# Row gathers that name fixed index columns instead of copied ones, in a hybrid attention, delta-rule and expert layer

## Chip, cores and metric

One NeuronCore of a Trainium2 chip. The metric is the device time of the program in microseconds (us). The engines are TensorE (PE), VectorE (DVE), ScalarE (ACT), GpSimd (POOL) and SyncE (SP); transfers run on 16 DMA engines.

## What is computed

One layer over 1024 tokens of width 1024, in fp32: layer norm; a mixing part (sliding-window attention and a gated delta rule) with a residual and a second layer norm; then a sparse expert part, and a last layer norm. The expert part is what the change touches. For each token it picks 8 x 16 = 128 rows out of 16384, takes those rows of `expert_u` for dot products with the token, and adds the same rows of `expert_v` with the results as weights:

```python
expert = i1 * N_KEYS + i2                     # (tokens, 8 heads, 16)
gates = jax.nn.softmax(best, axis=-1)
...
u = jnp.take(expert_u, et, axis=0)            # (128 tokens, 128 slots, 1024)
act = jax.nn.gelu(jnp.einsum('tkd,td->tk', u, xt), approximate=False) * gt
return jnp.einsum('tk,tkd->td', act, jnp.take(expert_v, et, axis=0))
```

Each row is 4 KB, so a token reads 1 MB and all 1024 tokens read 1.07 GB.

## The kernel before

The tokens are cut into T = 8 tiles of P = 128, one token a partition. A first stage (up to about 540 us) makes the first layer norm and the input projections of all tiles. A second stage then does for each tile the mixing part and the routing, in NPIECE = 49 pieces, and the gathers of its expert rows. The pieces of tile t + 1 are dealt out between the gathers of tile t, engine by engine, by tables written out by hand (`VECTOR_AT`, `TENSOR_AT`, `SCALAR_AT`); the pieces of tile 0 run alone ahead of the first gather (at about 617 us), and the last tile's gathers run with no pieces beside them.

A tile has SLOTS = 128 rows for each token, in NGROUP = 32 groups of GS = 4. One gather (`indirect_dma_start`) is issued by POOL and reads one row for each of 128 tokens, 512 KB. There are four buffers for U rows and four for V rows. In step s POOL issues, for k = 0 to 3 in turn, the U gather of group s and the V gather of group s - 1 into buffer k (L822, L827), each behind a wait until the buffer is free (`g_ufree[k]` at L820, `g_vfree[k]` at L825). DVE makes the dot product of each U row with the token (L1708), which frees the U buffer; ACT makes the gelu of the four dots (L1292) and frees the fourth; DVE multiplies with the gate (L1722). The V rows are added by weight: in most groups buffers 0 and 1 by PE, with diagonal matrices that ACT writes (L1286, L1130), and buffers 2 and 3 by DVE (L1714). Who adds a row frees its buffer. Each engine runs its instructions in the order in which they are written.

The indices of a tile are made by DVE in the last piece (n == 48), which waits for `g_indexfree`, writes `eidx_n` and raises `g_tile`. POOL (`next_tile`, L846) waits for `g_tile`, copies `eidx_n` to `eidx` (L849) and raises `g_indexfree`. A gather takes its index column from a small buffer: ahead of each step POOL copies four columns of `eidx` to `ixu` (L831) and the four of the group before to `ixv` (L834), waiting for each copy. The steps run in a loop over j with two steps in its body (L841) inside a loop over tiles (L859). At the end of a tile the last V columns are copied (L862), then the new tile's list (L849), then its first U columns (L853).

Of the kernel before, what the change touches and what calls it, by code (L numbers as in the profile page):

```python
# [17 lines left out]
P = 128  # L18
S = 1024
D = 1024  # L20
T = S // P
# [6 lines left out]
SLOTS = PH * TOPK  # L28
# [10 lines left out]
GS = 4  # L39
NGROUP = SLOTS // GS  # L40
# [72 lines left out]
def build(nc, consts, x, ln_in_g, ln_in_b, w_in, conv_w, a_sinks, b_a_log, b_dt_bias, b_norm_w, w_out,  # L113
          ln1_g, ln1_b, w_query, sub_keys, expert_u, expert_v, ln2_g, ln2_b, out):
    fp32, u32 = mybir.dt.float32, mybir.dt.uint32
# [3 lines left out]
    with ctx:  # L119
        def sb(name, shape, dt=fp32, c=ctx):  # L120
            return c.enter_context(nc.sbuf_tensor(name, shape, dt))
# [3 lines left out]
        def sem(name):  # L125
            return scope[0].enter_context(nc.semaphore(name))
# [4 lines left out]
        s_pool = sem("s_pool")  # L131
# [446 lines left out]
        b = ExitStack()  # L578
# [54 lines left out]
        eidx_n = sb("eidx_n", [P, SLOTS], u32, c=b)  # L633
        egate_n = sb("egate_n", [P, SLOTS], c=b)

        U = sb("U", [P, GS, D], c=b)
        V = sb("V", [P, GS, D], c=b)
        eidx = sb("eidx", [P, SLOTS], u32, c=b)
        egate = sb("egate", [P, SLOTS], c=b)
        ixu = sb("ixu", [P, 2, GS], u32, c=b)  # L640
        ixv = sb("ixv", [P, 2, GS], u32, c=b)
        dots = sb("dots", [P, 2, GS], c=b)
        gl = sb("gl", [P, 2, GS], c=b)
        dg = sb("dg", [P, 2, GS, P], c=b)
# [86 lines left out]
        g_u = [sem(f"g_u{k}") for k in range(GS)]  # L731
        g_v = [sem(f"g_v{k}") for k in range(GS)]
        g_ufree = [sem(f"g_ufree{k}") for k in range(GS)]
        g_vfree = [sem(f"g_vfree{k}") for k in range(GS)]
# [27 lines left out]
        rows = bass.IndirectOffsetOnAxis  # L762

        with nc.Block() as block:
# [48 lines left out]

            @block.gpsimd
            def _(pool):
                def fetch(par, u, v):

                    for k in range(GS):
                        if u:
                            pool.wait_ge(g_ufree[k], 1)  # L820
                            pool.sem_inc(g_ufree[k], -1)  # L821
                            pool.indirect_dma_start(U[:, k, :], None, expert_u[0],  # L822
                                                    rows(ap=ixu[:, par, k:k + 1], axis=0)).then_inc(g_u[k], 16)
                        if v:
                            pool.wait_ge(g_vfree[k], 1)  # L825
                            pool.sem_inc(g_vfree[k], -1)
                            pool.indirect_dma_start(V[:, k, :], None, expert_v[0],  # L827
                                                    rows(ap=ixv[:, 1 - par, k:k + 1], axis=0)).then_inc(g_v[k], 16)

                def step(s, par):  # L830
                    nc.gpsimd.tensor_copy(ixu[:, par, :], eidx[:, bass.ds(s * GS, GS)]).then_inc(s_pool, 1)  # L831
                    pool.wait_ge(s_pool, 1)
                    pool.sem_inc(s_pool, -1)  # L833
                    nc.gpsimd.tensor_copy(ixv[:, 1 - par, :], eidx[:, bass.ds(s * GS - GS, GS)]).then_inc(s_pool, 1)  # L834
                    pool.wait_ge(s_pool, 1)
                    pool.sem_inc(s_pool, -1)
                    fetch(par, True, True)

                def steps():

                    with pool.Fori(0, NGROUP // 2 - 1) as j:  # L841
                        step(2 * j + 1, 1)
                        step(2 * j + 2, 0)
                    step(NGROUP - 1, 1)

                def next_tile():  # L846
                    pool.wait_ge(g_tile, 1)
                    pool.sem_inc(g_tile, -1)  # L848
                    nc.gpsimd.tensor_copy(eidx[:, :], eidx_n[:, :]).then_inc(s_pool, 1)  # L849
                    pool.wait_ge(s_pool, 1)  # L850
                    pool.sem_inc(s_pool, -1)
                    pool.sem_inc(g_indexfree, 1)
                    nc.gpsimd.tensor_copy(ixu[:, 0, :], eidx[:, 0:GS]).then_inc(s_pool, 1)  # L853
                    pool.wait_ge(s_pool, 1)
                    pool.sem_inc(s_pool, -1)

                next_tile()
                fetch(0, True, False)
                with pool.Fori(0, T - 1) as t:  # L859
                    steps()  # L860

                    nc.gpsimd.tensor_copy(ixv[:, 1, :], eidx[:, SLOTS - GS:SLOTS]).then_inc(s_pool, 1)  # L862
                    pool.wait_ge(s_pool, 1)
                    pool.sem_inc(s_pool, -1)
                    next_tile()
                    fetch(0, True, True)
                steps()
                nc.gpsimd.tensor_copy(ixv[:, 1, :], eidx[:, SLOTS - GS:SLOTS]).then_inc(s_pool, 1)
                pool.wait_ge(s_pool, 1)
                pool.sem_inc(s_pool, -1)  # L870
                fetch(0, False, True)

            @block.tensor
            def _(pe):
# [1012 lines left out]
```

## Time and profile before

| | us |
|---|---|
| median of 3 runs | 4302.2 (4296.01 to 4318.66) |
| span of the profiled execution | 4299.7 |
| DVE, PE, POOL, ACT busy | 2684.1, 2796.3, 2539.3, 652.9 |
| gathers on POOL: 1024 U, 1024 V | 1189.4 and 1151.0 busy |
| copies on POOL | 187 busy |
| DVE waited for U rows | 737.9, in 442 waits |

The span is what the profiler saw from the first to the last instruction of one execution. Views of this execution show groups of instructions by source line (busy time, mean, idle time ahead of them and what ended it), waits by releaser, the instructions in order of time, and busy time by stretch. On POOL, "issue" as releaser means that nothing that the profile shows was waited for, and "POOLq L821" that the last thing ahead was a row of POOL's own sequencer at that line, a semaphore wait included.

### The profile page before, as it was taken

The page shows a single profiled execution, that of the slowest core. Times are in us where ns is not written, and L with a number is a line of the kernel's source. Part 1 is how long each engine was busy: PE and PEld are TensorE (multiplying, and loading weights), DVE is VectorE, ACT ScalarE, POOL GpSimd, SP SyncE. Part 2 cuts the span into 40 slices and gives each one's busy share as a digit, 9 for nine tenths or more (in the row PEclk, how much of TensorE's full clock was granted, in tenths as well). Part 3 has the DMA queues.
Part 4 walks back from the last instruction along what each step waited for, and adds up shares of the span by engine and source line. Part 5 has one row for each costly group of instructions (what it writes and reads, how often), then busy time and mean ns, then how long its engine had stood idle before and what let it go on. Part 6 is the DMA issues. An engine that isn't in the chain of part 4 may idle for free. (4 is left out here: it accounts for less than half of the span.)

```text
span 4299.7 us, 36977 instructions
## 1 busy us (share of the span) xinstructions
PE 2796.3 (65%) x8621; PEld 1470.1 (34%) x8621; DVE 2684.1 (62%) x5500; ACT 652.9 (15%) x1407; POOL 2539.3 (59%) x2582
## 2 busy tenths in 40 slices
PE   5997726676567656675567657765666566764444
PEld 2444523342244324242334224332434233521111
DVE  3121267677666867586766766686768776776555
ACT  2122102111211112111211121111211121111000
POOL 1000017667666766677667766676667766777775
PEclk9998767788777878788788867787878877887666
DMA  3224128888888888888888888888898888889997
GB/s 118 73 78 161 58 78 309 307 309 290 307 294 310 307 308 291 317 306 293 306 308 294 300 304 294 309 305 304 288 330 314 294 306 313 304 300 319 321 317 268
DMA packets 365654, 1172.84 MB, mean 273 GB/s; under 512 B 45285, under 2 KB 86294, under 8 KB 364442
## 3 DMA queue, kind: packets, MB, share of 16 engines
q0 software_dynamic: 294912, 1073.87, 71.3%
q1 hardware_dynamic: 66090, 81.05, 5.6%
q10 hardware_dynamic: 4464, 15.76, 1.0%
q8 instruction: 75, 1.23, 0.1%
q14 instruction: 113, 0.93, 0.1%
HBM read 1150.59 MB, written 19.96 MB: 272 GB/s over the span
## 5 line engine op out<-in xcount | busy, mean ns | idle before, releaser
L1130 PE MATMUL bank<-V,dg 128*128 128x512 f32 x2412 | 1518.5, 787 | 1168.8 <-PEq L1123 822.2
L1708 DVE CUSTOM_DVE_ANT_0 U<-U,h1c 128x1024 f32<-128x1024 f32 x1024 | 1253.2, 1227 | 933.4 <-DMA U<-in_expert_u,ixu 737.9
L827 POOL DMA_INDIRECT V<-in_expert_v,ixv x1024 | 1151.0, 1124 | 568.6 <-POOLq L821 296.5
L822 POOL DMA_INDIRECT U<-in_expert_u,ixu x1024 | 1189.4, 1161 | 493.2 <-issue 202.8
L1130 PEld LDWEIGHTS bank<-V,dg 128*128 128x128 f32 x2412 | 578.1, 253 | 2060.5 <-issue 1537.6
L1714 DVE SCALAR_TENSOR_TENSOR acc<-V,gl,acc 128x1024 f32<-128x1024 f32 x421 | 540.2, 1283 | 69.1 <-DMA V<-in_expert_v,ixv 61.0
L849 POOL COPY eidx<-eidx_n 128x128 uint32<-128x128 uint32 x8 | 4.2, 529 | 567.2 <-POOLq L848 566.9
L1286 ACT ACTIVATE dg<-C,gl 128x128 f32<-128x128 f32 x603 | 202.1, 392 | 683.5 <-ACTq L1284 615.4
L1292 ACT ACTIVATE gl<-dots 128x4 f32<-128x4 f32 x256 | 52.6, 206 | 1663.4 <-ACTq L1290 1652.7
L425 PE MATMUL bank<-hT,wbuf 128*128 128x512 f32 x704 | 304.1, 595 | 0.0
L970 PE MATMUL bank<-arena,wq 128*128 128x128 f32 x2048 | 255.5, 290 | 14.8 <-PEq L1104 8.9
L970 PEld LDWEIGHTS bank<-arena,wq 128*128 128x128 f32 x2048 | 251.3, 206 | 20.0 <-issue 19.7
L425 PEld LDWEIGHTS bank<-hT,wbuf 128*128 128x128 f32 x704 | 134.3, 191 | 169.0 <-issue 169.0
L379 DVE SCALAR_TENSOR_TENSOR ybuf<-bank,cw,ybuf 128x1023 f32<-128x1023 f32 (+2 forms) x36 | 46.1, 1281 | 201.0 <-DVEq L377 195.2
L945 PE MATMUL bank<-wo,arena 128*128 128x512 f32 x224 | 116.4, 664 | 25.5 <-PEq L1083 24.2
L834 POOL COPY ixv<-eidx 128x4 uint32 (+1 forms) x248 | 87.9, 354 | 69.5 <-POOLq L833 53.7
L1292 ACT ACT_TABLE_LOAD x50 | 64.2, 1283 | 209.3 <-ACTq L1290 206.6
L831 POOL COPY ixu<-eidx 128x4 uint32 (+1 forms) x248 | 91.4, 368 | 1.0
L1708 DVE DVE_READ_ACCUMULATOR2_ANT dots<- 128x1 f32 x1024 | 84.0, 82 | 0.0
L893 PE MATMUL bank<-raw 128*128 128x128 f32 x256 | 60.8, 325 | 27.5 <-PEq L890 22.4
L945 PEld LDWEIGHTS bank<-wo,arena 128*128 128x128 f32 x224 | 45.7, 211 | 85.2 <-issue 84.1
L894 PE MATMUL bank<-raw 128*128 128x128 f32 x320 | 67.1, 309 | 6.8 <-issue 3.4
(253 smaller groups left out, 2408.4 us busy)
## 6 DMA issues: line engine op xcount, KB each, us to landing
wo<-in_w_out SPq DMA_DIRECT2D x56, 512.0 KB
U<-in_expert_u,ixu POOLq DMA_INDIRECT x1024
V<-in_expert_v,ixv POOLq DMA_INDIRECT x1024
proj_dram<-obuf ACTq DMA_DIRECT2D x21, 512.0 KB, 2.6
raw<-proj_dram SPq DMA_DIRECT2D x8, 1344.0 KB
wbuf<-in_w_in SPq DMA_DIRECT2D x18, 512.0 KB, 3.8
wq<-in_w_query SPq DMA_DIRECT2D x4, 2048.0 KB, 18.0
xin<-in_x SPq DMA_DIRECT2D x8, 512.0 KB, 5.4
```

The costliest lines, as they stand in the source:

```text
L425: last = nc.tensor.matmul(banks[u][:, 512 * half:512 * half + 512], wbuf[:, u, k, :], hT[:, k, 512 * half:512 * half + 512], start=k == 0, ...
L822: pool.indirect_dma_start(U[:, k, :], None, expert_u[0], rows(ap=ixu[:, par, k:k + 1], axis=0)).then_inc(g_u[k], 16)
L827: pool.indirect_dma_start(V[:, k, :], None, expert_v[0], rows(ap=ixv[:, 1 - par, k:k + 1], axis=0)).then_inc(g_v[k], 16)
L831: nc.gpsimd.tensor_copy(ixu[:, par, :], eidx[:, bass.ds(s * GS, GS)]).then_inc(s_pool, 1)
L834: nc.gpsimd.tensor_copy(ixv[:, 1 - par, :], eidx[:, bass.ds(s * GS - GS, GS)]).then_inc(s_pool, 1)
L945: return nc.tensor.matmul(b0[:, 512 * n:512 * n + 512], yT[:, k, :], w[:, 512 * n:512 * n + 512], start=k == 0, stop=k == KD - 2)
L970: last = nc.tensor.matmul(o, wq[:, k, i * P:(i + 1) * P], h1T[:, k, :], start=k == 0, stop=k == KD - 1)
L1130: ins = nc.tensor.matmul(acc_ps[:, 512 * n:512 * n + 512], dg[:, 1 - par, k, :], V[:, k, 512 * n:512 * n + 512], start=first and k == 0, s ...
L1286: nc.scalar.activation(dg[:, 1 - par, k, :], ident, ACT.Copy, scale=gl[:, 1 - par, k:k + 1]).then_inc(g_diag, 1)
L1292: nc.scalar.activation(gl[:, par, :], dots[:, par, :], ACT.Gelu).then_inc(g_gelu, 1)
L1708: return nc.vector.tensor_tensor_reduce(out=U[:, k, :], in0=U[:, k, :], in1=h1c[:, :], scale=1.0, scalar=0.0, op0=ALU.mult, op1=ALU.add, a ...
L1714: return nc.vector.scalar_tensor_tensor(out=acc[:, :], in0=V[:, k, :], scalar=gl[:, 1 - par, k:k + 1], in1=acc[:, :], op0=ALU.mult, op1=AL ...
```

## The change

`eidx` gets two halves by tile, and each gather names its column of `eidx` itself. The buffers `ixu` and `ixv` and all copies into them go. For the column to be a fixed address, a tile's 31 steps after the first are written out, and the loop over tiles becomes one over pairs of tiles (`T // 2 - 1` = 3 turns) whose body holds two tiles with the halves 1 and 0. The order of the gathers, the waits for free buffers and the semaphores they raise are the same.

```diff
-        eidx = sb("eidx", [P, SLOTS], u32, c=b)
+        eidx = sb("eidx", [P, 2, SLOTS], u32, c=b)
-        ixu = sb("ixu", [P, 2, GS], u32, c=b)
-        ixv = sb("ixv", [P, 2, GS], u32, c=b)
...
-                def step(s, par):
-                    nc.gpsimd.tensor_copy(ixu[:, par, :], eidx[:, bass.ds(s * GS, GS)]).then_inc(s_pool, 1)
-                    pool.wait_ge(s_pool, 1)
-                    pool.sem_inc(s_pool, -1)
-                    nc.gpsimd.tensor_copy(ixv[:, 1 - par, :], eidx[:, bass.ds(s * GS - GS, GS)]).then_inc(s_pool, 1)
-                    pool.wait_ge(s_pool, 1)
-                    pool.sem_inc(s_pool, -1)
-                    fetch(par, True, True)
...
+                def u_row(e, s, k):
+                    pool.wait_ge(g_ufree[k], 1)
+                    pool.sem_inc(g_ufree[k], -1)
+                    c = s * GS + k
+                    pool.indirect_dma_start(U[:, k, :], None, expert_u[0],
+                                            rows(ap=eidx[:, e, c:c + 1], axis=0)).then_inc(g_u[k], 16)
...
+                def next_tile(e):
                     pool.wait_ge(g_tile, 1)
                     pool.sem_inc(g_tile, -1)
-                    nc.gpsimd.tensor_copy(eidx[:, :], eidx_n[:, :]).then_inc(s_pool, 1)
+                    nc.gpsimd.tensor_copy(eidx[:, e, :], eidx_n[:, :]).then_inc(s_pool, 1)
                     pool.wait_ge(s_pool, 1)
                     pool.sem_inc(s_pool, -1)
                     pool.sem_inc(g_indexfree, 1)
-                    nc.gpsimd.tensor_copy(ixu[:, 0, :], eidx[:, 0:GS]).then_inc(s_pool, 1)
-                    pool.wait_ge(s_pool, 1)
-                    pool.sem_inc(s_pool, -1)
...
+                def tile_rows(e):
+                    for s in range(1, NGROUP):
+                        for k in range(GS):
+                            u_row(e, s, k)
+                            v_row(e, s - 1, k)
+
+                def tile_after(e):
+                    next_tile(e)
+                    for k in range(GS):
+                        u_row(e, 0, k)
+                        v_row(1 - e, NGROUP - 1, k)
+                    tile_rows(e)
+
+                next_tile(0)
+                for k in range(GS):
+                    u_row(0, 0, k)
+                tile_rows(0)
+                with pool.Fori(0, T // 2 - 1):
+                    tile_after(1)
+                    tile_after(0)
+                tile_after(1)
+                for k in range(GS):
+                    v_row(1, NGROUP - 1, k)
```

## Rows read from the trace of the kernel before

**Rows 1.** The page's DMA queues: packets, MB, share of 16 engines' span.

```profile
q0 software_dynamic: 294912, 1073.87, 71.3%
```

**Rows 2.** Busy time by stretch: length, engines' busy us (instructions), PE's clock, DMA share, GB/s.

```profile
2463.00:2932.00 469.00, 311.67 (x982) 166.46 (x981) 323.00 (x673) 73.25 (x169) 314.39 (x321) 0.78 0.87 301
2932.00:3391.00 459.00, 302.11 (x984) 161.62 (x983) 322.85 (x674) 73.44 (x169) 316.00 (x321) 0.81 0.88 309
3849.00:4260.00 411.00, 188.11 (x263) 71.53 (x262) 236.53 (x350) 31.77 (x97) 304.77 (x311) 0.70 0.90 316
```

**Rows 3.** Timeline in the last tile: start, us, instruction, idle time before and releaser.

```profile
4099.91 0.19 POOL L831 COPY ixu<-eidx 128x4 uint32 x1
4100.35 0.19 POOL L834 COPY ixv<-eidx 128x4 uint32 x1 [0.24 <-POOLq L833]
4101.44 1.08 POOL L822 DMA_INDIRECT U<-in_expert_u,ixu  x1 [0.90 <-POOLq L826]
...
4104.14 1.20 POOL L822 DMA_INDIRECT U<-in_expert_u,ixu  x1 [0.30 <-issue]
...
4105.65 0.93 POOL L827 DMA_INDIRECT V<-in_expert_v,ixv  x1 [0.30 <-issue]
4106.57 1.22 DVE L1708 CUSTOM_DVE_ANT_0 U<-U,h1c 128x1024 f32<-128x1024 f32 x1 [0.83 <-DMA U<-in_expert_u,ixu]
4106.88 1.73 POOL L822 DMA_INDIRECT U<-in_expert_u,ixu  x1 [0.30 <-issue]
...
4110.15 0.94 POOL L822 DMA_INDIRECT U<-in_expert_u,ixu  x1 [0.30 <-issue]
...
4110.42 1.22 DVE L1708 CUSTOM_DVE_ANT_0 U<-U,h1c 128x1024 f32<-128x1024 f32 x1 [2.55 <-DMA U<-in_expert_u,ixu]
...
4112.46 0.20 POOL L831 COPY ixu<-eidx 128x4 uint32 x1
...
4113.03 1.23 DVE L1708 CUSTOM_DVE_ANT_0 U<-U,h1c 128x1024 f32<-128x1024 f32 x1 [1.37 <-DMA U<-in_expert_u,ixu]
```

**Rows 4.** Waits in the last tile, 3849 to 4260 us: total, times, longest.

```profile
DVE U L1708 <- DMA U<-in_expert_u,ixu: 152.9, 93, 3.2
```

**Rows 5.** Groups on POOL in the last tile: busy us, mean ns | idle before, releasers.

```profile
L822 POOL DMA_INDIRECT U<-in_expert_u,ixu x125 | 156.5, 1252 | 57.3 <-POOLq L826 27.8 <-issue 27.7 <-POOLq L821 1.8
L827 POOL DMA_INDIRECT V<-in_expert_v,ixv x124 | 135.2, 1090 | 42.1 <-issue 32.6 <-POOLq L821 7.4 <-POOLq L826 2.1
L831 POOL COPY ixu<-eidx 128x4 uint32 (+1 forms) x31 | 7.5, 241 | 0.1
L834 POOL COPY ixv<-eidx 128x4 uint32 (+1 forms) x31 | 7.3, 236 | 7.5 <-POOLq L833 6.8 <-issue 0.7
```

**Rows 6.** Groups on POOL in the middle tile, 2463 to 2932 us.

```profile
L827 POOL DMA_INDIRECT V<-in_expert_v,ixv x128 | 148.3, 1158 | 81.4 <-POOLq L821 45.5 <-issue 33.2 <-POOLq L826 2.7
L822 POOL DMA_INDIRECT U<-in_expert_u,ixu x128 | 144.8, 1131 | 63.4 <-issue 26.5 <-POOLq L821 20.4 <-POOLq L826 16.2
L831 POOL COPY ixu<-eidx 128x4 uint32 (+1 forms) x31 | 11.5, 371 | 0.1
L834 POOL COPY ixv<-eidx 128x4 uint32 (+1 forms) x31 | 9.2, 295 | 8.8 <-POOLq L833 6.8 <-issue 2.0
L849 POOL COPY eidx<-eidx_n 128x128 uint32<-128x128 uint32 x1 | 0.3, 289 | 0.3 <-POOLq L848 0.3
L862 POOL COPY ixv<-eidx 128x4 uint32<-128x4 uint32 x1 | 0.2, 191 | 0.0
L853 POOL COPY ixu<-eidx 128x4 uint32<-128x4 uint32 x1 | 0.2, 186 | 0.2 <-POOLq L851 0.2
```

**Rows 7.** Waits in the middle tile: total, times, longest.

```profile
DVE U L1708 <- DMA U<-in_expert_u,ixu: 86.6, 47, 6.2
POOL V L827 <- POOLq L821: 45.5, 18, 7.0
DVE U L1708 <- issue: 11.1, 11, 6.9
```

**Rows 8.** Timeline in the first tile: a V gather that waits for its buffer.

```profile
765.72 0.94 POOL L827 DMA_INDIRECT V<-in_expert_v,ixv  x1 [6.67 <-POOLq L821]
```

**Rows 9.** The stretch of 25 us in the last tile that moved most.

```profile
3882.00:3907.00 25.00, 13.34 (x21) 4.82 (x19) 15.66 (x22) 3.04 (x8) 17.59 (x19) 0.73 0.96 343
```

**Rows 10.** Timeline of DVE at its loop over tiles: the first dot after the jump.

```profile
2519.99 1.23 DVE L1708 CUSTOM_DVE_ANT_0 U<-U,h1c 128x1024 f32<-128x1024 f32 x1 [6.93 <-issue]
```

More of the change, by code:

```diff
@@ L815, in _ @@
             def _(pool):
[L816 to L828, printed above, removed]
@@ L830, in step @@
-                def step(s, par):
-                    nc.gpsimd.tensor_copy(ixu[:, par, :], eidx[:, bass.ds(s * GS, GS)]).then_inc(s_pool, 1)
-                    pool.wait_ge(s_pool, 1)
-                    pool.sem_inc(s_pool, -1)
-                    nc.gpsimd.tensor_copy(ixv[:, 1 - par, :], eidx[:, bass.ds(s * GS - GS, GS)]).then_inc(s_pool, 1)
-                    pool.wait_ge(s_pool, 1)
-                    pool.sem_inc(s_pool, -1)
-                    fetch(par, True, True)
[L839 to L844, printed above, removed]
@@ L846, in next_tile, with v_row @@
-                def next_tile():
+                def u_row(e, s, k):
[4 more added lines that the diff above has]
+                                            rows(ap=eidx[:, e, c:c + 1], axis=0)).then_inc(g_u[k], 16)
+                def v_row(e, s, k):
+                    pool.wait_ge(g_vfree[k], 1)
+                    pool.sem_inc(g_vfree[k], -1)
+                    c = s * GS + k
+                    pool.indirect_dma_start(V[:, k, :], None, expert_v[0],
+                                            rows(ap=eidx[:, e, c:c + 1], axis=0)).then_inc(g_v[k], 16)
@@ L852, in next_tile @@
                     pool.sem_inc(g_indexfree, 1)
-                    nc.gpsimd.tensor_copy(ixu[:, 0, :], eidx[:, 0:GS]).then_inc(s_pool, 1)
-                    pool.wait_ge(s_pool, 1)
-                    pool.sem_inc(s_pool, -1)
[L857 to L871, printed above, removed]
+                def tile_rows(e):
[19 more added lines that the diff above has]
+                    v_row(1, NGROUP - 1, k)
             @block.tensor
```

## The prediction

> **What bounds the kernel now.** Read first the page's queue line: the gathers of expert rows move 1073.87 MB on queue q0, whose packets take 71.3% of the sixteen DMA engines' span [rows 1]. Then the busy table by stretch [rows 2]: seven tiles (617 to 3849 us) run gathers beside the next tile's mixing and routing, the eighth (3849 to 4260 us) runs gathers alone. In neither does an engine look full: in a middle tile of 469 us DVE is busy 323.0, POOL 314.4, PE 311.7, the DMA engines 0.87; in the last tile DVE has 236.5 of 411 and the DMA engines 0.90. But POOL is fuller than its busy time says. In the timeline of the last tile [rows 3] each gather runs 0.93 to 1.73 us and the next begins 0.30 us behind it, released by nothing ("issue"). Behind the fourth V gather come the two index copies, 0.24 us apart, and behind them 0.90 us, not 0.30, until the next U gather. So POOL is never free there, and DVE waits for rows: 152.9 us in 93 waits in the last tile [rows 4]. There POOL sets the pace: the group period is 411/31 = 13.26 us; 4 x 1.252 + 4 x 1.090 = 9.37 in gathers [rows 5], 8 x 0.30 = 2.40 in gaps, 1.32 for the copies (below), 13.09 together, 0.17 left for true waits.
>
> In the seven overlapped tiles it is shared. In the middle tile POOL's gathers take 148.3 + 144.8 = 293.1 us, the idle time ahead of them 81.4 + 63.4 = 144.8 [rows 6]. Of this 256 x 0.30 = 77 is the fixed gap and 32 x 0.60 = 19 is what the copies add to theirs, which leaves 49 us in which POOL waited for a buffer to be freed; 45.5 us of the idle time stands under one releaser ahead of V gathers [rows 7]. A plain case is the V gather that starts at 765.72 after 6.67 us [rows 8]: PE frees V buffers 0 and 1 and was at work on the next tile. DVE, in turn, waited 86.6 us for U rows in this tile [rows 7]. So the chain goes back and forth: POOL, transfer, DVE or PE, buffer free, POOL.
>
> **What is removed, and its cost.** Per group: two copies of 128x4 with their semaphore waits. In the middle tile 0.371 + 0.295 = 0.67 us of copies, 8.8/31 = 0.28 between them [rows 6], and 0.90 - 0.30 = 0.60 of longer gap [rows 3]: 1.55 us a pair. In the last tile 0.241 + 0.236 = 0.48, 7.5/31 = 0.24 [rows 5], and 0.60: 1.32. At a tile boundary three copies become one: the copy from L862 (0.2) and the one from L853 (0.2 and 0.2 of idle) go too [rows 6], about one pair more, so I count 32 pairs for each of the seven tiles and 31 for the last. If all of it were on the path: 224 x 1.55 + 31 x 1.32 = 388 us. That is the ceiling, and not the forecast.
>
> **Last tile.** POOL's period without the pair is 13.26 - 1.32 = 11.94 us. The next thing that is late is the transfer. A group moves 8 x 0.524 = 4.19 MB; the stretch ran at 316 GB/s with share 0.90 [rows 2], which is 351 GB/s at share 1, hence 11.95 us a group. The best 25 us in it had 343 GB/s at 0.96 [rows 9], 357 at share 1. A queue that must be always full costs something, so I take 0.98 of 351: 12.2 us. The time from the start of a U gather to its dot says the same: 5.13, 6.28 and 6.15 us in one group [rows 3], it grows within a group, and the copies' pause lets it recover. Gain 13.26 - 12.2 = 1.06 us, x 31 = 33 us. Bounds: 31 x 0.4 = 12 (the ceiling of rival 2) and 31 x 1.32 = 41.
>
> **The seven tiles.** What counts are the pairs on the chain. I followed it back through the timelines of POOL, DVE and PE from the last gather of each tile: along POOL while a gather starts at its fixed gap (0.30, or 0.90 behind the copies, as in [rows 3]); over to the engine that frees the buffer where it starts later (as in [rows 8]); from DVE or PE back to POOL where a dot or a product had waited for its rows (the dots at 4106.57 and 4110.42 in [rows 3] are such). It crosses 83 of the 224 pairs, between 7 and 17 in a tile. A pair on the chain is worth less than 1.55: a copy alone needs 0.19 to 0.20 [rows 3], so 0.67 - 0.39 = 0.28 us of a pair is stretching. DVE work beside it is the likely reason: the gather at 4106.88 ran 1.73 us with a dot already running, the one at 4110.15, where the dot began after it, 0.94 [rows 3]. Without copies about half of this falls on the gather that comes there instead; I take 1.40. 83 x 1.40 = 116 us. Then chains that run close beside take over, and the transfer queue fills: 0.87 of the 469 us tile is 408 us of DMA time, and shortened by 17 us the tile is at 0.90, the share at which the last tile runs; this costs a part of it. I take three quarters, 87 us. Bounds: 83 x 1.55 = 129 above if my count is right, and a third (30 us) below; if the count is short by half, 190.
>
> **What is added and moved.** The second index buffer alternates by tile, so the copy from L849 stays, eight times, 0.29 us each [rows 6]; its wait is that of before. What is queued behind it on POOL is the new tile's first U gather and the old tile's last V gathers, on which DVE and PE wait; DVE hands over the list at the same place in its own order, and L849 had 0.3 us of idle time ahead of it [rows 6], so if POOL comes earlier than DVE this wait grows by at most the about 1.5 us that one group gained: 7 x 0 to 1.5, cost 0 to 10, and I take 0, since DVE comes earlier too. The order and number of gathers, and of every DMA, is the same; SP's, ACT's and PE's queues aren't touched.
>
> The code of POOL grows from a loop over two groups to one over two tiles, walked three times, with two jumps back over 512 gathers. No row of POOL shows such a jump. The nearest is DVE's own loop over the tiles, whose first dot after the jump stood 6.93 us for "issue" [rows 10]. For POOL: 2 x 0 to 7 us, part of it behind gathers already in its queue; I take 5 in all. The Trainium skill, page "Runtime: NRT & Kernel Launch", section "Instruction fetch mechanics", says that a sequencer fetches ahead in sequence and that a taken branch to a target outside its window of two blocks stalls it for a fetch; by that rule the change trades a loop that stays inside the window for one that doesn't, and straight code costs nothing. The row of the jump agrees with it; that straight code is free on POOL, no row shows.
>
> **Sum.** Against the profiled span of 4299.7, which stands 2.5 us (0.06%) below the median of 4302.2: -87 - 33 + 5 = -115. From the median: **4187 us**, 2.7% less.
>
> **Rivals.**
> 1. More pairs pass on (chance 0.17). The chain has many near equals, and POOL's earlier issue may lift waits that my walk gives to DVE or PE. For it: DVE's 86.6 us of waits in a tile of which I use 12. Against: POOL waits 49 us for buffers. 130 of 224 pairs at 1.40 is 182, with the last tile 33: 215 less 5, 4092.
> 2. The transfer, or DVE and PE, take over at once (0.19). If 325 GB/s is what random rows give when asked without pause, the last tile's period is 13.26 x 316/325 = 12.89, a gain of 11 us, and the tiles, at 301 to 309 GB/s already, keep a third of mine, 30: 4302 - 41 + 5 = 4266. For it: share 0.87 to 0.90 now. Against: 343 GB/s in 25 us.
> 3. No change that can be told (0.08): all of the seven tiles' pairs are hidden and the last tile gives 11: 4291. The form in which the change does not do what it says would land here too: copies left in the code. The diff leaves one per tile, so I give that nothing of its own.
> 4. Slower (0.06): POOL stands at blocks of straight code as DVE does at its jump. One stop of 6.93 us [rows 10] in every eight groups is 32 x 6.93 = 222 us against a gain of 115: 4409. It decides from 3.6 us a stop on (115/32). Against: of DVE's 11 "issue" waits in the middle tile, 11.1 us in all, the longest is 6.9 [rows 7], so its hundreds of straight instructions cost at most 4.2 us a tile.
>
> **How the numbers follow.** My forecast (4150 to 4225) has 0.50, the rivals 0.17, 0.19, 0.08 and 0.06. A measurement of this kernel can tell about 0.5%, 21.5 us, from no change. Faster by more: 0.50 + 0.17 + 0.19 = 0.86; same 0.08; slower 0.06. The range takes in the first rival up to its own value and most of the second's: 4095 to 4268, and leaves out the ends.
>
> **What would show it.** Copies on POOL: 8, no more. Gaps ahead of all U gathers 0.30 as ahead of V gathers; group period in the last tile about 12.2, DMA share there 0.97 or more, GB/s near 343; time from U gather to dot longer than 6.3 us there. In a middle tile about 450 us, DVE's waits for U rows down from 86.6 to about 75, and POOL's true waits up from 49 us to about 80. Two stops of POOL at the new jump. I am wrong if POOL's gathers get longer by more than 0.15 us, if "issue" gaps of microseconds stand on POOL away from the jump, or if the last tile keeps its 13.26 us.

## The result

The changed kernel took 4183.81 us (median, 4181.41 to 4185.75) against 4299.1 us for the kernel before (its fourth run lowers the 4302.2 that stands ahead): ratio 0.9727, with a 95% interval of 0.97 to 0.9754, in which the quotient of the two medians, 0.9732, lies too. The prediction said 4187. The profiled execution has a span of 4179.9 us, 119.8 less than before.

Groups of the page of the changed kernel (busy us, mean ns | idle before, releaser), for the whole execution:

```profile
L1695 DVE CUSTOM_DVE_ANT_0 U<-U,h1c 128x1024 f32<-128x1024 f32 x1024 | 1252.3, 1226 | 825.3 <-DMA U<-in_expert_u,eidx 609.3
L825 POOL DMA_INDIRECT V<-in_expert_v,eidx x1024 | 1166.9, 1140 | 768.0 <-POOLq L816 480.5
L818 POOL DMA_INDIRECT U<-in_expert_u,eidx x1024 | 1211.8, 1183 | 396.3 <-issue 244.2
L831 POOL COPY eidx<-eidx_n 128x128 uint32<-128x128 uint32 x8 | 2.4, 297 | 564.9 <-POOLq L830 564.9
```

Eight copies are left on POOL. The same dots on DVE, 1252 us of them, waited 609.3 us for U rows where it had been 737.9, and POOL stands 768.0 us ahead of V gathers where it had stood 568.6.

Busy time by stretch of the changed kernel, two overlapped tiles and the last one (columns as in [rows 2], which they answer):

```profile
2844.00:3293.00 449.00, 294.02 (x980) 158.30 (x980) 321.85 (x673) 73.25 (x169) 294.37 (x257) 0.82 0.87 314
3293.00:3740.00 447.00, 300.06 (x981) 161.40 (x981) 320.73 (x672) 73.34 (x169) 295.59 (x257) 0.81 0.87 312
3741.00:4139.00 398.00, 184.41 (x264) 70.35 (x263) 238.36 (x351) 31.75 (x97) 306.04 (x248) 0.71 0.91 327
```

POOL in the last tile of the changed kernel, to set against [rows 5]:

```profile
L818 POOL DMA_INDIRECT U<-in_expert_u,eidx x124 | 159.5, 1286 | 40.4 <-issue 32.3 <-POOLq L816 5.9 <-POOLq L823 2.1
L825 POOL DMA_INDIRECT V<-in_expert_v,eidx x124 | 146.9, 1185 | 52.6 <-issue 30.2 <-POOLq L816 20.9 <-POOLq L823 1.5
```

And POOL in the middle tile (2394 to 2843 us), to set against [rows 6], with DVE's wait there against [rows 7]:

```profile
L818 POOL DMA_INDIRECT U<-in_expert_u,eidx x128 | 144.9, 1132 | 52.1 <-issue 29.0 <-POOLq L816 17.1 <-POOLq L823 6.1
L825 POOL DMA_INDIRECT V<-in_expert_v,eidx x128 | 143.7, 1123 | 108.6 <-POOLq L816 65.4 <-issue 28.6 <-POOLq L823 14.6
```

```profile
DVE U L1695 <- DMA U<-in_expert_u,eidx: 69.7, 36, 6.5
```

The reader is to see two things. In the middle tile the gathers are as long as they were (288.6 us, 293.1 before) and their idle time is 160.7 us; less 77 of fixed gaps, POOL now waits 84 us for free buffers where it had waited 49. So 35 us of the 50 that the copies gave back there (32 x 1.55) went into such waits. In the last tile the gathers themselves are longer: 1.236 us in the mean, 1.171 before.

To compare kernels, the table gives for each profiled execution the time from the first U gather of tile 0 to that of tile 7 (seven tiles), and from there over the next 31 groups (last tile). The letters stand for chips. B and C are two different ones; C was used twice, once before B and once after it. Of A, where the pair of the result ran, it isn't known which chip it was, and it may be B. A and B gave the changed kernel the same ratio; C did not, and that matters below. Each stretch in the table is of one execution; equal copies in the last tile of two kernels on C gave 408.8 and 417.9 us there, so differences of a few us between such stretches say little.

| kernel | chip | median us | ratio to before (95%) | seven tiles | last tile |
|---|---|---|---|---|---|
| before | A | 4299.1 | 1 | 3231.8 | 410.8 |
| changed | A | 4183.81 | 0.9727 (0.97 to 0.9754) | 3124.7 | 398.7 |
| changed again | B | 4185.49 | 0.9707 (0.9674 to 0.974) | 3131.4 | 393.4 |
| unused buffers | B | 4182.82 | 0.9704 (0.9668 to 0.974) | 3128.1 | 394.0 |
| last-tile copies, moved | B | 4193.1 | 0.9732 (0.9702 to 0.9761) | 3120.0 | 408.3 |
| short dots | B | 3952.1 | 0.9178 (0.9144 to 0.9212) | 2922.2 | 358.6 |
| changed, third time | C | 4301.44 | 0.9932 (0.9908 to 0.9957) | 3242.5 | 397.8 |
| written out, with copies | C | 4292.54 | 0.9931 (0.9911 to 0.9951) | 3208.7 | 418.5 |
| copies without drain | C | 4312.11 | 0.9975 (0.9949 to 1.0) | 3253.7 | 402.4 |
| the same, moved | C | 4310.93 | 0.9968 (0.9943 to 0.9993) | 3258.5 | 401.6 |
| last-tile copies | C | 4322.87 | 0.9998 (0.9975 to 1.002) | 3252.0 | 408.8 |
| the same again | C | 4327.1 | 1.0 (0.997 to 1.003) | 3256.7 | 417.9 |
| one copy, looped | C | 4259.5 | 0.9862 (0.9813 to 0.9911) | 3187.9 | 401.0 |
| four U, then four V | C | 4419.09 | 1.023 (1.0184 to 1.0276) | 3307.4 | 445.8 |

The kernel before took 4310.85 us on B, and 4322.65 and 4327.98 on C beside the two sets of runs.

### The profile page after: what moved, and what is told of

Its sections match the earlier page's. It is cut to its first block and busy times, and to the rows that moved or that the text cites. A ratio compares the mean times of both kernels' runs of the same rounds, so it can differ in the third digit from the quotient of the medians.

```text
span 4179.9 us, 35217 instructions
## 1 busy us (share of the span) xinstructions
PE 2734.9 (65%) x8621; PEld 1444.9 (35%) x8621; DVE 2681.4 (64%) x5500; ACT 653.2 (16%) x1407; POOL 2392.1 (57%) x2070
## 5 line engine op out<-in xcount | busy, mean ns | idle before, releaser
L1117 PE MATMUL bank<-V,dg 128*128 128x512 f32 x2412 | 1474.0, 767 | 1131.5 <-PEq L1110 866.1
L1695 DVE CUSTOM_DVE_ANT_0 U<-U,h1c 128x1024 f32<-128x1024 f32 x1024 | 1252.3, 1226 | 825.3 <-DMA U<-in_expert_u,eidx 609.3
L825 POOL DMA_INDIRECT V<-in_expert_v,eidx x1024 | 1166.9, 1140 | 768.0 <-POOLq L816 480.5
L818 POOL DMA_INDIRECT U<-in_expert_u,eidx x1024 | 1211.8, 1183 | 396.3 <-issue 244.2
L1117 PEld LDWEIGHTS bank<-V,dg 128*128 128x128 f32 x2412 | 565.3, 247 | 1992.8 <-issue 1772.6
L831 POOL COPY eidx<-eidx_n 128x128 uint32<-128x128 uint32 x8 | 2.4, 297 | 564.9 <-POOLq L830 564.9
L1695 DVE DVE_READ_ACCUMULATOR2_ANT dots<- 128x1 f32 x1024 | 84.1, 82 | 0.0
L881 PE MATMUL bank<-raw 128*128 128x128 f32 x320 | 67.2, 309 | 6.8 <-PEq L877 6.8
L1667 DVE TENSOR_TENSOR arena<-arena 128x800 f32<-128x800 f32 x64 | 63.5, 992 | 9.4
L1670 DVE TENSOR_REDUCE arena<-arena 128x16 f32<-128x800 f32 x64 | 63.1, 986 | 9.3
```

Of the source, the lines that this page charges most:

```text
L818: pool.indirect_dma_start(U[:, k, :], None, expert_u[0], rows(ap=eidx[:, e, c:c + 1], axis=0)).then_inc(g_u[k], 16)
L825: pool.indirect_dma_start(V[:, k, :], None, expert_v[0], rows(ap=eidx[:, e, c:c + 1], axis=0)).then_inc(g_v[k], 16)
L881: last = nc.tensor.matmul(g[2][:, h * P:(h + 1) * P], Pm[:, h, :], XT[:, h, :], start=True, stop=True)
L1117: ins = nc.tensor.matmul(acc_ps[:, 512 * n:512 * n + 512], dg[:, 1 - par, k, :], V[:, k, 512 * n:512 * n + 512], start=first and k == 0, s ...
L1667: nc.vector.tensor_tensor(eq, eq, cid[:, h, :].unsqueeze(1).to_broadcast([P, TOPK, NCAND]), ALU.mult).then_inc(s_dve, 1)
L1695: return nc.vector.tensor_tensor_reduce(out=U[:, k, :], in0=U[:, k, :], in1=h1c[:, :], scale=1.0, scalar=0.0, op0=ALU.mult, op1=ALU.add, a ...
```

## The experiments

The theory was that of the prediction: the copies cost what they add to POOL's chain, where POOL's chain is the late one. The rivals were that the written-out code is the gain, that only the fight of the copies with DVE counts, and that the transfers were the next limit.

**Written out, with copies.** Both copies and their waits ahead of each written-out step, into buffers that nobody reads:

```diff
+                def pair(e, s):
+                    nc.gpsimd.tensor_copy(ixu[:, s % 2, :], eidx[:, e, s * GS:s * GS + GS]).then_inc(s_pool, 1)
+                    pool.wait_ge(s_pool, 1)
+                    pool.sem_inc(s_pool, -1)
+                    nc.gpsimd.tensor_copy(ixv[:, 1 - s % 2, :], eidx[:, e, s * GS - GS:s * GS]).then_inc(s_pool, 1)
+                    pool.wait_ge(s_pool, 1)
+                    pool.sem_inc(s_pool, -1)
                 def tile_rows(e):
                     for s in range(1, NGROUP):
+                        pair(e, s)
```

> The changed kernel with both index copies and their waits put back ahead of each written-out step (248 pairs; the copied buffers are read by nobody). Theory (the copies are the whole cost): the time of before less the boundary copies, 4285 to 4300 us. Rival (the written-out, static code is the gain, the copies were cheap): 4184 to 4220 us.

Measured: 4292.54 us, inside the theory's 4285 to 4300. But the kernel before took 4322.65 beside it, not 4302, and the ratio of 0.9931 is lower than the theory's 0.996 to 0.9995. Written-out code gives 0.7% there, of which the boundary copies, also left out here, are a part. The last tile has 418.5 us. The changed kernel on the same chip, further down, took 4301.44 (0.9932): on C, putting all copies back cost nothing over the whole kernel. This edit was not timed on A or B, so it does not show there what the copies are worth in the seven tiles.

**Copies without drain.** The same copies, but the wait for both stands at the end of the step:

```diff
                         for k in range(GS):
                             u_row(e, s, k)
                             v_row(e, s - 1, k)
+                        pool.wait_ge(s_pool, 2)
+                        pool.sem_inc(s_pool, -2)
```

> The changed kernel with both copies put back ahead of each step, but the wait for them only at the end of the step, five gathers later, so that the sequencer runs on. It takes the execution of the copies (0.38 to 0.67 us a pair) apart from the drain of the sequencer (0.24 between them and 0.60 behind them). Theory (time of POOL's chain, whatever makes it): 0.4 of the loss comes back, 4225 to 4235 us. Rival (only the drain costs, the copies slip in between): within 10 us of 4184. Second rival (only the copies' fight with DVE costs): 4270 or more.

Measured: 4312.11 us, far from the first two numbers, and slower than with the full waits. By the number it falls to the second rival (4270 or more); its last tile, 402.4 us where the full waits have 418.5, speaks against that one. Taken with the next one, it made clear that something else was at work.

**Copies in the last tile alone.** `pair` only in the last call of `tile_rows`.

> The changed kernel with both copies and waits put back in the last tile's 31 steps alone. As the trace of the changed kernel shows it, the last tile gained 12 us and the seven others 107: 4196 us. As the prediction had it, 33 us in the last tile: 4217 us.

Measured: 4322.87 us, as before the change, where both theories had a number below 4220. The last tile had its 408.8 us, but the seven tiles, whose code is that of the changed kernel, took 3252.0 us against its 3124.7.

**One copy, looped.** The kernel before with its loop, and one copy of the eight columns from s * GS - GS on. The gathers take their columns from the new buffer `ix`; those lines are not shown:

```diff
-                    nc.gpsimd.tensor_copy(ixu[:, par, :], eidx[:, bass.ds(s * GS, GS)]).then_inc(s_pool, 1)
-                    pool.wait_ge(s_pool, 1)
-                    pool.sem_inc(s_pool, -1)
-                    nc.gpsimd.tensor_copy(ixv[:, 1 - par, :], eidx[:, bass.ds(s * GS - GS, GS)]).then_inc(s_pool, 1)
+                    nc.gpsimd.tensor_copy(ix[:, par, :], eidx[:, bass.ds(s * GS - GS, 2 * GS)]).then_inc(s_pool, 1)
                     pool.wait_ge(s_pool, 1)
                     pool.sem_inc(s_pool, -1)
...
```

> The kernel before with its loop over two groups kept, and one copy of eight index columns ahead of each step in the place of two of four. It saves 0.3 us of a copy and 0.25 to 0.3 us between the two, and keeps the 0.60 behind them. Theory: 0.55 to 0.6 us of 1.55 a pair, 4253 to 4260 us. Rival (the loop or the drain is what costs): 4290 us or more.

Measured: 4259.5 us beside 4322.65, 63 us, where 42 to 49 were expected from 4302; the ratio expected, 0.989 to 0.990, lies within the interval. It is a cut of the copies with no written-out code, and it is the fastest kernel on C. So one copy with its wait is worth 1.4% without any change of the loop. How much of the 2.7% of A and B is the second copy and how much the straight code was not taken apart there.

**Changed again, and unused buffers.** The changed kernel itself on B, beside it the same with `ixu` and `ixv` allotted and unused.

> The changed kernel itself again, beside the next three on one chip. The copies put back in the last tile alone had cost 139 us against the changed kernel of another chip, where 12 were expected, so the size of the gain itself is in question. Theory A (the gain belongs to the change): a ratio of 0.97 to 0.975 to the kernel before. Theory B (the gain hangs on the chip): 0.985 to 1.0.

> The changed kernel with the two index buffers still allotted, used by nobody, so that the eight tensors behind them (dots, gl, dg, acc, h1c and so on) lie 64 bytes further on in each partition, where the run with copies in the last tile had them. If the place of these tensors is what took the gain away: 4300 or more. If not: as the changed kernel, within 10 us.

Measured: 4185.49 and 4182.82 us, 0.9707 and 0.9704. The place of the tensors does nothing that can be told.

**Last-tile copies, moved.** The copies in the last tile alone, their buffers behind all others.

> Copies in the last tile's 31 steps alone, as before, but with their two buffers allotted behind all others, so that every tensor lies where the changed kernel has it. If places decide: the changed kernel and 12 us. If the clock of TensorE decides, which stood at 0.65 of full in group 12 of the tiles with the loss and at 0.84 without it, and which such a detail doesn't reach: anything between 4190 and 4320, with the loss in groups 12, 22 and 24 of the tiles where the clock is low.

Measured: 4193.1 us, 8 to 10 more than the two above; the last tile went from 393.4 and 394.0 to 408.3 us, and the seven tiles, with 3120.0 us, did not grow. So the copies cost 14 to 15 us in the last tile on one and the same chip.

**Short dots.** DVE's dots over 128 columns; seven eighths of each dot product are left out.

```diff
-                    return nc.vector.tensor_tensor_reduce(out=U[:, k, :], in0=U[:, k, :], in1=h1c[:, :], scale=1.0, scalar=0.0,
+                    return nc.vector.tensor_tensor_reduce(out=U[:, k, 0:P], in0=U[:, k, 0:P], in1=h1c[:, 0:P], scale=1.0, scalar=0.0,
```

> The changed kernel with DVE's dot products over 128 of the 1024 columns (part of the computation is left out: seven eighths of each dot product), which takes most of the work away that stretches POOL's gathers and leaves every gather as it is. It shows what the transfers alone allow in the last tile. If transfers set the changed kernel's 12.86 us a group there: it stays at 12.5 or more. If POOL's stretched gathers do (1.24 us each against 0.94 alone): POOL's own bound falls to 8 x 1.24 = 9.9 and the period goes to the transfer's limit, 11.7 to 12.2 by the 351 GB/s of the prediction. DVE is relieved too, so the seven tiles shorten also, by an unknown size.

Busy time and POOL's groups in its last tile:

```profile
3535.00:3893.00 358.00, 183.79 (x260) 68.07 (x260) 126.64 (x349) 31.76 (x97) 246.72 (x249) 0.74 0.97 363
```

```profile
L818 POOL DMA_INDIRECT U<-in_expert_u,eidx x125 | 124.6, 997 | 39.8 <-issue 25.1 <-POOLq L816 7.4 <-POOLq L823 7.1
L825 POOL DMA_INDIRECT V<-in_expert_v,eidx x124 | 123.6, 997 | 72.4 <-POOLq L816 47.4 <-issue 22.9 <-POOLq L823 2.1
```

The same gathers now take 0.997 us, the period is 358.6/31 = 11.57 us, and the DMA engines are at 0.97 with 363 GB/s. So the transfers allow 11.6 us, and the changed kernel's 12.86 was not theirs. What stretches POOL's gathers is DVE's work on the dots: it is all that was cut.

**The changed kernel a third time, and the last-tile copies again,** on C.

> The changed kernel a third time, as the reference of this call's chip. As on the two chips so far: a ratio of 0.970 to 0.973.

> The kernel with copies in the last tile alone and their buffers ahead of dots, gl and the others, which took 4323 us where its twin with the buffers behind them took 4193, each on its own chip. In the slow one PE's last product of a step signalled DVE about 6 us late, at the same instruction of five of six tiles. If this belongs to the kernel (the places of its tensors): 4310 to 4330 again. If it belonged to that chip: 4190 to 4200.

Measured: 4301.44 and 4327.1 us, 0.9932 and 1.0. The second lies in the range of the theory that the kernel is at fault, but the changed kernel itself, to the letter the one of A and B, loses three quarters of its gain on C. So the loss belongs to that chip together with this code, and not to the last tile's copies. It lies in the seven tiles: 3242.5 us where B has 3131.4, while the last tile is as it was, 397.8. In those tiles DVE stands still at the same three instructions of a tile: in 17 of 21 cases it waits more than 2.5 us there, and in no case in the changed kernel on A and B. One of them, on C (timeline: start, us, instruction, idle before and releaser):

```profile
3105.15 1.13 PE L881 MATMUL bank<-raw 128*128 128x128 f32 x8 [0.85 <-issue]
...
3106.83 1.28 DVE L1701 SCALAR_TENSOR_TENSOR acc<-V,gl,acc 128x1024 f32<-128x1024 f32 x1
...
3114.01 0.69 DVE L1386 TENSOR_TENSOR raw<-raw,bank 128x512 f32<-128x512 f32 x1 [5.91 <-DVEq L1385]
3115.00 0.77 PE L1030 MATMUL bank<-arena,raw 128*128 128x128 f32 x2 [8.72 <-PEq L1028]
```

and the same place in the same tile on B:

```profile
3035.58 1.13 PE L881 MATMUL bank<-raw 128*128 128x128 f32 x8 [0.85 <-PEq L877]
...
3037.17 1.28 DVE L1701 SCALAR_TENSOR_TENSOR acc<-V,gl,acc 128x1024 f32<-128x1024 f32 x1
...
3038.81 0.69 DVE L1386 TENSOR_TENSOR raw<-raw,bank 128x512 f32<-128x512 f32 x1 [0.36 <-DVEq L1385]
3039.80 0.77 PE L1030 MATMUL bank<-arena,raw 128*128 128x128 f32 x2 [3.08 <-PEq L1028]
```

DVE waits at L1385 for PE's eight products of L881. They have the same modelled length in both, 1.13 us, but on C the semaphore that the last one raises is recorded at 3113.9 us, 7.6 us behind the product's modelled end; on B at its end. The two other places are L1709 in group 22, waiting for ACT's gelu, and L1695 in group 24, waiting for a U row. Together the three are 12 us a tile longer than on B, 84 of the 111 us.

At L1709 the trace shows the stop arise on TensorE. These are PE's rows before the stop in the third tile on C, all of one line, with no other product between them:

```profile
1843.63 9.60 PE L957 MATMUL bank<-arena,wq 128*128 128x128 f32 x76
1853.40 0.58 PE L957 MATMUL bank<-arena,wq 128*128 128x128 f32 x3 [0.17 <-issue]
...
1856.25 0.40 PE L957 MATMUL bank<-arena,wq 128*128 128x128 f32 x2 [0.92 <-issue]
1857.68 1.10 PE L957 MATMUL bank<-arena,wq 128*128 128x128 f32 x4 [1.03 <-issue]
...
1860.57 8.70 PE L957 MATMUL bank<-arena,wq 128*128 128x128 f32 x59 [0.33 <-issue]
```

and the same products on B:

```profile
1809.73 19.04 PE L957 MATMUL bank<-arena,wq 128*128 128x128 f32 x169
```

On B the products run in one piece. On C they come in twos to fours, 1.4 us apart, with gaps that nothing in the profile ended. ACT's copy of their results (L1256) starts only at 1864.80, the gelu behind it in ACT's order at 1865.71, and DVE's L1709, 5.97 us idle, at 1866.07. Over the whole execution PE and its weight loads stand 80.2 us in 144 such "issue" gaps ahead of this product line in the changed kernel on C, and 65 to 103 us in the four other kernels with stops. On A and B it is 13 us in 8 gaps. On C it is 28.4 us with full copies and waits, 16.3 with one copy looped and 13.4 with four U, then four V.

TensorE's granted clock is lower in several of these stretches, but not in all. Busy time of the group with L1386 in the second and the sixth tile, first on B, then on C:

```profile
1228.50:1240.10 11.60, 7.23 (x40) 5.88 (x38) 8.97 (x16) 0.88 (x3) 7.81 (x9) 0.85 1.00 401
3032.00:3043.40 11.40, 7.47 (x37) 6.19 (x38) 8.83 (x16) 0.79 (x2) 7.64 (x8) 0.77 1.01 392
```

```profile
1245.90:1263.10 17.20, 9.99 (x37) 7.97 (x37) 8.89 (x16) 0.69 (x2) 7.66 (x8) 0.62 0.85 335
3101.70:3118.60 16.90, 7.33 (x37) 6.05 (x37) 8.78 (x16) 0.79 (x2) 7.60 (x8) 0.76 0.85 341
```

In the sixth tile the clock's share is 0.77 on B and 0.76 on C (between the levels of 1.2 and 2.4 GHz), and the group took 11.4 and 16.9 us. So a lower clock is not what makes the stop. What is shown: stops at L1709 and in group 24 occur on C in five kernels whose POOL code is written out and doesn't drain at each step (changed, last-tile copies twice, copies without drain twice). The one at L1386 stands in three of these, in one tile of the first run of the copies without drain, and not in its moved twin. A sixth kernel of this kind, four U, then four V, has none of the three on C, so written-out code alone does not make them. With full copies and waits, and with one copy looped, DVE is idle 0.4 us ahead of L1386 and not at all ahead of L1709 in every tile; ahead of the dot in group 24 the first waits more than 2.5 us in four tiles, up to 6.3. What keeps TensorE from its next product is open. The loading of instructions is the obvious guess, but no packet of the two instruction queues starts during any of the changed kernel's five stops at L1386.

**Copies without drain, moved.**

> Both copies ahead of each step with the wait for them at the end of the step, as before, but with their buffers behind all other tensors. The first run of this edit had 4312 us, with the same stops of DVE in groups 12, 22 and 24 of a tile as the kernel with copies in the last tile alone. Without those stops the theory of POOL's time expects 4225 to 4235 (0.4 of the loss of 115), the rival that only the drain of the sequencer costs 4184 to 4195.

Measured: 4310.93 us, beside 4301.44 for the changed kernel on the same chip: 9 us for all copies. This one has stops too, so it is to be read against that kernel, and the ranges expected without stops can't be tested on the whole time. In the last tile, where there are none, the copies without drain cost 3.8 and 4.6 us (401.6 and 402.4 to 397.8). Those with drain cost 20.1, 20.7 and 11.0 us on C (417.9, 418.5 and 408.8). So some six to eight tenths of a pair's cost there is the drain, that is, the sequencer standing until POOL is empty. The theory, by which the copies keep 0.4 of their cost without the drain, would ask for 4.4 to 8.3 us; it comes out too high in the mean and isn't excluded by the smallest. The rival that only the drain costs is the nearer one.

**Four U, then four V.** In each step, and at the start of each tile (not shown), first all U gathers, then all V gathers:

```diff
                         for k in range(GS):
                             u_row(e, s, k)
+                        for k in range(GS):
                             v_row(e, s - 1, k)
...
```

> The changed kernel with the order of a step's gathers changed: four U rows, then four V rows, in the place of U and V by turns. In the changed kernel POOL stands 480 us ahead of V gathers, up to 11 us at a time, with U gathers behind them whose buffers are free. If that wait is what makes DVE wait 609 us for U rows: 20 to 80 us faster than the changed kernel, 4105 to 4165. If PE and DVE then wait as long for V rows: no change.

Measured: 4419.09 us, 2.3% slower than before and 2.7% slower than the changed kernel on that chip: neither of the two outcomes expected. Its waits in the last tile:

```profile
PEld bank L1119 <- DMA V<-in_expert_v,eidx: 280.4, 40, 10.7
PE bank L1119 <- DMA V<-in_expert_v,eidx: 249.0, 30, 9.9
DVE acc L1703 <- DMA V<-in_expert_v,eidx: 167.4, 29, 6.8
POOL U L818 <- POOLq L823: 110.4, 30, 5.3
```

DVE does a dot and then an addition by turns, in its written order. With V rows issued last, its first addition waits for them and holds up the dots whose rows are there; DVE's waits for V rows in that tile are 167.4 us, 16.4 in the changed kernel. The waits of POOL ahead of V gathers were no free time to be had by issuing U earlier.

## Why the prediction was right, and where not

The time, 4187 for 4183.8, is nearer than its terms: the gain was put 20 us too small in the seven tiles and 21 too large in the last one, and 5 us of cost did not come. The first two errors cancel, which is luck.

*What bounds the kernel.* Right in kind: the copies stood on POOL's chain. The looped kernel with one copy, with nothing written out, gained 1.4% on C. Putting both back into the last tile of the written-out code took it from 393.4 to 408.3 us on B. For the seven tiles no run puts them back where there are no stops, so that all of their gain is the copies' is argued from the waits and not shown.

*The seven tiles.* Forecast 87 us, measured 3231.8 - 3124.7 = 107. A tile came out at 450 (about 450), DVE's waits for U rows at 69.7 (about 75), POOL's true waits at 84 (about 80). The count of 83 pairs of 224 on the chain is not measured by any run; it is consistent with the result, which makes 107/83 = 1.29 us a pair, under the 1.40 of a full one. If the count is right, the discount by a quarter for near chains and a fuller queue was too large, and a tenth would have done (116 to 107). The DMA share stayed at 0.87, where it was to reach 0.90, since the same share moved more: 314 GB/s for 301.

*The last tile.* Forecast 33 us, measured 12; over four profiles without copies and five with both (before among them) it is 396.0 against 412.9, 17 us. Two steps failed. The first: "The next thing that is late is the transfer", at 12.2 us a group. With short dots the same transfers ran at 11.57. The step took the best 25 us of the trace, 343 GB/s, for near the most; the short dots held 363 through a whole tile. The second, which hid the first: POOL's own period was put at 11.94 by taking the copies away from a gather time of 9.37 us. The gathers grew to 4 x 1.286 + 4 x 1.185 = 9.88, and true waits from 0.17 to (93.0 - 74.4)/31 = 0.60; 9.88 + 2.40 + 0.60 = 12.88, the measured 12.86. The prediction had put half of the copies' stretching on the gathers in the seven tiles, and none in the last. DVE's work, still 7.7 us a group (238.36/31), now meets gathers all the time. The signs for the last tile failed with it: a share of 0.97 and 343 GB/s were named, and 0.91 and 327 came.

*The price of a pair.* The sum 0.67 + 0.28 + 0.60 counts idle time behind the copies as good as their busy time. That was right, and more than right: without the drain the copies' own time is nearly hidden (3.8 to 4.6 us, against 11 to 21 with it). The prediction didn't see why. In the last tile of the changed kernel the sequencer's rows have four waits for free buffers 0.57 us apart, at 4001.44 to 4003.15 us, and the four gathers behind them start at 4003.48 to 4008.30. So the sequencer runs ahead, the gathers queue between it and the engine, and waits for a buffer are met early; each copy's wait empties that queue.

*What was added.* Nothing of it is seen on A. The wait for the new list grew by nothing (of the 564.9 us ahead of L831, 564.6 are the first tile's), and POOL shows no stop at its jump: its longest "issue" gap is 1.2 us (2.2 us on C). The two stops that were named as a sign did not come, and the 5 us of the sum were too many. The longer code is seen in the page alone: instruction queue q14 moved 147 packets, 1.20 MB, where it had moved 113, 0.93 MB.

*The rivals.* The second, transfers or consumers at once, and the third did not come true on A and B. But the second had the last tile right to the number (a period of 12.89 us and a gain of 11, for 12.86 and 12) and for the wrong reason: its 325 GB/s as the limit is refuted by the 363 of the short dots. On C the outcome, 0.9932, lies between those of the second (4266, 0.992) and the third (4291, 0.997), its interval takes in the second's alone, and it came by the reasons of neither: DVE waits in stops that it doesn't have in the rows of before. The fourth, stops in straight code, named about the right length (6.93 us a stop, for 3 to 7 us of DVE's idle time on C), and put them on POOL; none stood there. A part of its mechanism did come on C, on TensorE: gaps with no releaser inside a row of equal products. The prediction's ground against it, DVE's few "issue" gaps, came from another engine and from one trace.

## What to carry to other kernels

A short helper operation with a wait, ahead of a queue of slow ones, costs more by the queue that it empties than by its own time: look at the gap behind it, and first move its wait, which took most of the pair's cost away in the last tile here. Where an engine that seems free stretches another's instructions, cutting idle time on the second brings a part of it back as longer instructions. When an engine waits, follow the wait to the engine where equal instructions come with gaps that nothing ended. A gain of two or three per cent that comes from closer overlap of five engines should be timed on more than one chip; the mildest form of the change (one copy in the loop, 0.9862 on C) was the surest there.

## What was not expected of the hardware

One program ran at 0.9727, 0.9707 and 0.9932 of the kernel before on A, B and C, where the kernel before itself moved by 0.7% at most. On C, rows of equal products of TensorE broke up into twos to fours, with gaps of up to 1.1 us in the changed kernel that nothing ended. There too, a semaphore that rides on a product of TensorE was recorded up to 7.6 us behind the product's modelled end, and over 2 us behind at the same instruction in four of seven tiles (in five of seven, and by up to 8.0 us, in the kernel with the last tile's copies). In the one shown, the DMA share of the group was 0.85 for 1.01. And a gather of 512 KB took POOL 0.997 us beside short dots and 1.236 beside full ones, the transfers being the same.

The traces differ in a second way. That of the changed kernel holds 49938 semaphore updates on A and 49940 on B, and 39120 on C, so on C an update that is missing says nothing; in the stop shown DVE's own wait ends at 3113.91 us, right behind the recorded update. The trace of the kernel before has this trait as well (44151) and some of TensorE's gaps (23.8 us in 28 ahead of that product line). So the two traces of the result may come from different chips, and small differences between their rows are to be taken with care. The ratio on B, where both kernels were timed on one chip, doesn't hang on that.
